# A two-layer hybrid trunk in fp32: step sizes from x itself, head products interleaved in pairs, rotary partner rows copied by DMA

## The reference

```python
h = rmsnorm(x, ln1_g[l]);  proj = h @ w_in[l]
# A: differential attention, 4 heads x 2 components x 64; q and k of each:
q = partial_rope(rmsnorm(q, qk_norm_g[l, 0]), cos, sin)      # k likewise with [l, 1]
def partial_rope(x, cos, sin):                               # first 16 of the 64 dims turn
    x1, x2 = xr[..., :half], xr[..., half:]                  # half = 8
    rot = concat([x1 * c - x2 * s, x1 * s + x2 * c])
    return concat([rot, x[..., ROPE_DIM:]])
# C: S5, a complex diagonal state scan (8 blocks j of 128 states here)
# D: Mamba-2 with 4 heads x 64 and 4 chunks of 128 tokens:
dt = softplus(proj[..., OFF_M2DT:] + dt_bias)                # 4 step sizes per token
y = scores_with_decay @ x_dt + decayed_C @ entering_state    # per head and chunk
y = rmsnorm((y + d_skip * xs) * silu(z), norm_g)
```

## Time and profile before

| | |
|---|---|
| median of 3 runs | 1403.04 us (1402.85 to 1403.28) |
| profiled execution, its own time | 1402.84 us |
| its span | 1401.1 us |
| busy: PE, DVE, POOL, ACT | 1354.3, 924.5, 686.2, 503.7 us |
| granted TensorE clock, mean | 0.99 |
| granted clock from 157.5 to 170 us, mean | 0.73 |
| first qk mean product of layer 0 | at 149.46 us |

### The profile page before, as it was taken

One profiled execution on the slowest core, in us unless ns is written; L12 is line 12 of the kernel. 1 busy time (PEld: TensorE's weight loads), 2 busy tenths in 40 slices (PEclk: granted clock), 3 DMA queues, 4 the chain that ended last, 5 costly groups with the idle time before them and its releaser, 6 DMA issues.

```text
span 1401.1 us, 15858 instructions
## 1 busy us (share of the span) xinstructions
PE 1354.3 (97%) x6130; PEld 1058.0 (76%) x6130; DVE 924.5 (66%) x1239; ACT 503.7 (36%) x754; POOL 686.2 (49%) x370
## 2 busy tenths in 40 slices
PE   7999998899999999999999999989999999999999
PEld 4877566677788888888878765657778888888887
DVE  8879987666788506776237798966577772177730
ACT  5432334655332212323334324445562322123221
POOL 2836897114444444444456378941244444444442
PEclk9999999999999999999999999999999999999999
DMA  6321111113333322323233211111132333233332
GB/s 218 96 61 61 60 48 51 34 42 84 104 93 104 119 78 91 104 91 114 81 108 95 69 46 60 60 46 30 40 113 91 103 104 103 81 95 102 96 111 94
DMA packets 34091, 118.43 MB, mean 85 GB/s; under 512 B 3936, under 2 KB 4064, under 8 KB 34016
## 3 DMA queue, kind: packets, MB, share of 16 engines
q1 hardware_dynamic: 34016, 117.42, 26.6%
HBM read 114.26 MB, written 2.10 MB: 83 GB/s over the span
## 4 chain that ended last, share of the span: by engine, by line
PE 88%; DVE 9%; ACT 1%; issue 1%; POOL 1%; DMA 0%; SPq 0%; DVEq 0%; POOLq 0%
PE bank L423 26%; PE bank L436 25%; PE bank L428 24%; PE bank L490 1%; PE bank L425 1%; PE bank L636 1%; PE bank L499 1%; PE bank L465 1%; PE bank L595 1%; PE bank L597 1%; PE bank L617 1%; PE bank L627 1%; PE bank L449 1%; DVE bank L1055 1%; DVE ml L1061 1%
## 5 line engine op out<-in xcount | busy, mean ns | idle before, releaser
L318 POOL TENSOR_TENSOR wl<-raw,wh 128x1024 fp32r<-128x1024 f32 (+3 forms) x208 | 501.2, 2410 | 633.1 <-ACT wh L771 390.7
L423 PE MATMUL bank<-xl,wh 128*128 128x512 f32 x1152 | 303.3, 402 | 1.7 <-DVE xl L1022 1.1
L771 ACT ACTIVATE wh<-raw 128x1024 fp32r<-128x1024 f32 (+3 forms) x208 | 218.5, 1051 | 236.3 <-PE bank L428 204.1
L436 PE MATMUL bank<-xh,wl 128*128 128x512 f32 x1152 | 285.9, 390 | 0.0
L428 PE MATMUL bank<-xh,wh 128*128 128x512 f32 x1120 | 277.7, 390 | 0.0
L423 PEld LDWEIGHTS bank<-xl,wh 128*128 128x128 f32 x1152 | 215.7, 190 | 72.7 <-issue 25.3
L436 PEld LDWEIGHTS bank<-xh,wl 128*128 128x128 f32 x1152 | 216.0, 188 | 45.1 <-issue 0.3
L428 PEld LDWEIGHTS bank<-xh,wh 128*128 128x128 f32 x1120 | 211.2, 189 | 44.3
L1065 DVE TENSOR_TENSOR x<-x,bank 128x512 f32<-128x512 f32 x64 | 44.0, 688 | 225.1 <-PE bank L436 225.1
L423 PE MATMUL bank<-ml,wh 128*128 128x512 f32 x512 | 139.9, 401 | 0.0
L436 PE MATMUL bank<-mh,wl 128*128 128x512 f32 x512 | 127.5, 389 | 0.0
(11 more groups left out here) (275 smaller groups left out, 1497.2 us busy)
## 6 DMA issues: line engine op xcount, KB each, us to landing
raw<-in_w_gu SPq DMA_DIRECT2D x88, 512.0 KB, 3.5
raw<-in_w_in SPq DMA_DIRECT2D x52, 512.0 KB, 3.5
raw<-in_w_dn SPq DMA_DIRECT2D x32, 704.0 KB, 4.1
raw<-in_w_oe SPq DMA_DIRECT2D x16, 384.0 KB, 3.0
raw<-in_w_ol SPq DMA_DIRECT2D x16, 256.0 KB, 2.6
x<-in_x SPq DMA_DIRECT2D x8, 256.0 KB, 6.8
raw<-in_w_first SPq DMA_DIRECT2D x4, 512.0 KB, 4.8
out_x<-x SPq DMA_DIRECT2D x8, 256.0 KB, 5.1
```

The costliest lines, as they stand in the source:

```text
L318: tt(wl[:, p, 0:cols], raw[:, p, 0:cols], wh[:, p, 0:cols].bitcast(F32), ALU.subtract).then_inc(wl_full, 1)
L423: mm(bank[b][:, :], wh[:, p, k * P:(k + 1) * P], lo[:, k, :], start=(k == 0), stop=False)
L436: w = mm(bank[b][:, :], wl[:, p, k * P:(k + 1) * P], hi[:, k, :], start=False, stop=(k == K - 1))
L771: fn(wh[:, p, 0:cols], raw[:, p, 0:cols], ACT.Copy).then_inc(wh_full, 1)
```

## The change

dt now comes from unsplit fp32 x: `wdt` holds g1 times the weight, padded with zeros to 32 columns, and the eight products go to four column groups of bank 5; a 0/1 matrix `pick` adds the groups in the turn. `m2_apply` works on a pair of heads, one in each half of the columns, products of the two in turn: heads 0 and 1 after unit 12, heads 2 and 3 in the middle of unit 15 (`beside`). `m2_pair(l, 1)` and ACT's square for it move from s = 14 to s = 15. The q and k weights are reordered on the host so that the rotary rows of both components lie on partitions 48 to 79 with partners next to each other. SP copies them swapped from G into `partner[t % 2]`, two DMAs of 16 rows for each t, queued ahead of a weight load. DVE clears the two buffers and copies the sine table to bank 5 once in a layer; the rotary sum is then made in bank 4, where the mean stood, so it waits for ACT's Ln.

```diff
 SP, in weights(g):
+                s = g % (len(UNITS) // L) - 4
+                if 16 <= s < 24:
+                    sp.wait_ge(unit_out, unit_out_of(g // (len(UNITS) // L), s))
+                    for to, of in ((0, 1), (1, 0)):
+                        sp.dma_start(partner[s % 2][ROT0 + to:ROT1:2, :],
+                                     G[ROT0 + of:ROT1:2, s % 2, :]).then_inc(partner_in[s % 2], 16)
                 sp.dma_start(raw[:, g % 2, 0:cols], src[l, i]).then_inc(raw_full[g % 2], 16)
 PE:
-                for n, (a, b) in enumerate(((wdth, xl), (wdth, xh), (wdtl, xh))):
-                    for k in range(KD):
-                        w = mm(bank[5][0:M2H, :], a[:, k, :], b[:, k, :], start=(n == k == 0),
+                for k in range(KD):
+                    r = SH * (k % 4)
+                    w = mm(bank[5][r:r + SH, :], wdt[:, k, :], x[:, k, :], start=(k < 4), stop=(k >= 4))
...
-                    w = nc.tensor.transpose(bank[5][:, t * M2H:(t + 1) * M2H], G[0:M2H, 5, t * P:(t + 1) * P],
+                    w = mm(bank[5][:, t * M2H:(t + 1) * M2H], G[:, 5, t * P:(t + 1) * P], pick, start=True, stop=True)
...
+            def m2_apply(i):
+                pe.wait_ge(mix_ready, nth(mix_ready, 2))
...
+                heads = [(2 * i + e, slice(M2P * e, M2P * e + M2P), *m2buf[e]) for e in range(2)]
+                    for h, r, decayed, _ in heads:
+                        w = mm(bank[5][r, c], xbt[:, t, i, r], decayed[:, c], start=True, stop=(t == 0))
...
 PE, qk_mean(t):
-                claim(4, act_free[4])
+                claim(4, qk_done)
                 mm(bank[4][:, :], block1, G[:, 2, :], start=True, stop=True).then_inc(act_bank[4], 1)
-                claim(5, qk_done)
-                mm(bank[5][:, :], permg[:, t % 2, :], G[:, t % 2, :], start=True, stop=True).then_inc(dve_bank[5], 1)
 PE, beside(s):
-                    if s == 11:
-                        m2_apply(0)
+                    if s == 14:
+                        m2_apply(1)
 DVE, qk_finish(l, t):
                 own(stt(q, G[:, p, :], par_of(l, "qkg", p), cosT, MUL, MUL))
-                dve.wait_ge(dve_bank[5], nth(dve_bank[5]))
-                after(tt(bank[5][:, :], bank[5][:, :], sinT, MUL))
-                after(tt(bank[5][:, :], q, bank[5][:, :], ADD))
+                dve.wait_ge(partner_in[p], 32 * (4 * l + t // 2 + 1))
+                dve.wait_ge(act_free[4], nth(act_free[4]))
+                after(stt(bank[4][:, :], partner[p], par_of(l, "partg", p), bank[5][:, :], MUL, MUL))
+                after(tt(bank[4][:, :], q, bank[4][:, :], ADD))
                 dve.wait_ge(qk_rms, nth(qk_rms))
-                tt(q, bank[5][:, :], G[:, 3 + p, :], MUL).then_inc(qk_done, 1)
+                tt(q, bank[4][:, :], G[:, 3 + p, :], MUL).then_inc(qk_done, 1)
 DVE, s == 15:
+                        nc.vector.memset(partner[0], 0.0)
+                        nc.vector.memset(partner[1], 0.0)
+                        dve.wait_ge(yz_ready, 2 * (l + 1))
+                        own(copy(bank[5][:, :], sinT))
```

More of the change, by code:

```diff
@@ L20 @@
 ROPE = 16
+ROT0, ROT1 = QK - ROPE, QK + ROPE
 THETA = 500000.0
@@ L45 @@
 CONSTS, _o = {}, 0
-for _name, _n in [("ident", P), ("ones", P), ("tri", P), ("perm", P), ("block", P), ("cap", P)]:
+for _name, _n in [("ident", P), ("ones", P), ("tri", P), ("block", P), ("cap", P), ("pick", 4)]:
     CONSTS[_name] = slice(_o, _o + _n)
@@ L148, in build @@
         hst = sb("hst", [P, NQ - 1, M2H, M2P])
+        wdt = sb("wdt", [P, KD, SH], at=offsets["hst"])
         rot = sb("rot", [P, L, 2, SJ, NT])
         rho_all = sb("rho_all", [P, L, SJ])
-        permg = sb("permg", [P, 2, P])
+        partner1 = sb("partner", [P, T], at=offsets["hst"])
+        partner = (G[:, 5, :], partner1[:, :])
         par_all = sb("par_all", [P, L, NPAR])
@@ L207, in build @@
         em_full, em_high, mixed_ready = sem("em_full"), sem("em_high"), sem("mixed_ready")
+        partner_in = [sem(f"partner_in{p}") for p in range(2)]
         sqk_ready, qk_rms, qk_done, v_ready = [sem(n) for n in ("sqk_ready", "qk_rms", "qk_done", "v_ready")]
@@ L1076, in parameters @@
             def parameters(l):
-                w = par_of(l, "wdt", 0, KD * M2H)
-                copy(flat(wdth[:]), w)
+                w = par_of(l, "wdt", 0, KD * M2H).rearrange("p (k h) -> p k h", k=KD)
+                after(nc.vector.memset(wdt[:, :, :], 0.0))
+                gain = par_of(l, "g1", 0, KD).unsqueeze(2).broadcast_to([P, KD, M2H])
                 ts(par_of(l, "subg"), par_of(l, "subg"), par_of(l, "oneml"), None, MUL)
+                ts(par_of(l, "partg"), par_of(l, "partg"), QK ** -0.5, None, MUL)
                 after(ts(par_of(l, "qkg"), par_of(l, "qkg"), QK ** -0.5, None, MUL))
[L1081 to L1085, removed]
+                tt(wdt[:, :, 0:M2H], w, gain, MUL).then_inc(wdt_ready, 1)
             def dt_scaled():
                 dve.wait_ge(dve_bank[5], nth(dve_bank[5]))
-                tt(G[0:M2H, 5, :], bank[5][0:M2H, :], rbc[0:M2H, :], MUL).then_inc(dve_free[5], 1)
+                tt(G[:, 5, :], bank[5][:, :], rbc[:, :], MUL).then_inc(dve_free[5], 1)
                 freed(dve_free[5])
@@ L1567, in _ @@
                         residual(o, o % 2)
+PAIRS = [d for i in range(ROPE // 2) for d in (i, i + ROPE // 2)]
+PLAIN = list(range(ROPE, QK))
+QK_ROWS = [(0, d) for d in PLAIN + PAIRS] + [(1, d) for d in PAIRS + PLAIN]
 def constants():
@@ L1580, in constants @@
     half = ROPE // 2
-    for b in range(2):
-        for i in range(half):
-            lo, hi = b * QK + i, b * QK + half + i
-            perm[hi, lo], perm[lo, hi] = -1, 1
-            cos[lo], cos[hi] = np.cos(ang[:, i]), np.cos(ang[:, i])
-            sin[lo], sin[hi] = np.sin(ang[:, i]), np.sin(ang[:, i])
-    c[:, CONSTS["perm"]] = perm
+    for row, (_, dim) in enumerate(QK_ROWS):
+        if dim < ROPE:
+            cos[row] = np.cos(ang[:, dim % half])
+            sin[row] = np.sin(ang[:, dim % half]) * (-1 if dim < half else 1)
     c[:, CONSTS["block"]] = r[:, None] // QK == r[None, :] // QK
+    c[:, CONSTS["pick"]] = r[:, None] % SH == np.arange(M2H)[None, :]
     c[:, CONSTS["cap"]] = np.where(r[None, :] >= r[:, None], 0.0, NEG)
@@ L1606, in layout @@
     for h in range(HEADS):
-        order += [w[:, :, h * P:(h + 1) * P], w[:, :, a + h * P:a + (h + 1) * P]]
+        rows = np.array([h * P + c * QK + d for c, d in QK_ROWS])
+        order += [w[:, :, rows], w[:, :, a + rows]]
     w_in = units(np.concatenate(order + [w[:, :, b:c]], axis=2))
@@ L1626, in layout @@
     put("g2", tiled(inp["ln2_g"]))
-    put("qkg", np.tile(inp["qk_norm_g"], (1, 1, 2)).transpose(0, 2, 1))
+    dims = np.array([d for _, d in QK_ROWS])
+    put("qkg", inp["qk_norm_g"][:, :, dims].transpose(0, 2, 1))
+    partner = np.where(dims < ROPE, (dims + ROPE // 2) % ROPE, dims)
+    put("partg", inp["qk_norm_g"][:, :, partner].transpose(0, 2, 1))
     put("subg", tiled(inp["subln_g"]))
```

48 lines of the change are left out of this document (19 added, 29 removed).

## The result

The changed kernel takes 1407.13 us (1406.01 to 1409.33), the kernel before 1403.05 in the same comparison: the ratio, estimated from all runs of both, is 1.0032, 95% interval 1.002 to 1.0044. It is 4 us slower, where I had forecast 11 us faster.

A forecast was written before the change was run, and what follows sets the result against it. PE bounds the kernel (97% busy), but DVE nearly fills the rotary stretch. Step sizes 3.1 plus 2.6 us from there on make 5.7 a layer, 11.4 in both: 1391.6 us forecast, own range 1388 to 1396, wider range 1383.5 to 1400.

The forecast's parts named there:

- dt: Input projection: eight plain fp32 products in four column groups take two rounds, 2.0 us, replacing 24 products of 5.56 us.
- the pair of heads: After unit 12: two heads' products, partly side by side in two column halves, take 1.9 us; bounds 1.67 and 3.34.
- the wait before `s5_in(2)`: Scan's second projection: PE arrives about 2 us before DVE's `s5_back(1)` has ended and waits.
- the second mean product's wait: Second rotary step: PE waits about 5 us for the last operation of DVE's `qk_finish(0)`; before, it waited 2.37 us.
- The permutation product: Rotary stretch: sixteen products removed, 6.9 us of PE time a layer, given no gain because DVE becomes the bound.
- DVE's convolutions start with the end of unit 3 and move along: Layer 0, behind the step sizes: DVE's convolutions follow PE's earlier finish, so the 3.1 us gain is kept.
- The price of a late copy: Rotary stretch, odd t: DVE ready at 200.0, copy landed at 200.9; two units take 17.4 us, 0.5 slower than before.
- partners in time: Rival, rotary stretch: copies never hold DVE, a pair takes 16.5 us, gain there 4.4 instead of 2.6, 1388.0 us; chance 0.19.
- First `qk_done`: Start of the rotary stretch: DVE's first `qk_done` comes 2.2 us earlier than the 161.2 before.
- the step sizes: Input projection of each layer: shorter products less a longer `dt_turn`, 5.56 - 2.0 - 0.5, net 3.1 us earlier.
- The clock: Rival: one more clock fall a layer behind PE's waits costs, say, 2.2 us, giving 1396; chance 0.13.
- The pairs: Heads in pairs, units 12 to 17: unit 17 starts about 2.5 us earlier; 1.1 if pairs do not overlap.

## Why the prediction was wrong

- **Prices of the PE work: right.** dt 1.9 us (2.0 forecast; four column groups do run side by side, and the estimate of 2.4 us for them was too high), the turn 0.8 (+0.5 net), the pair of heads 1.9 (1.9), the wait before `s5_in(2)` 1.78 (2), the second mean product's wait 5.0 (5). The permutation product was given nothing, and that holds: with the copies early, the kernel without it takes 1386.6 us and the one with it 1386.1. Those two differ in more than this product (the second also has the held-up pair for `permg`), so a small price could hide there.
- **"DVE's convolutions start with the end of unit 3 and move along": this step failed, and cost some 7 us.** They did start earlier (unit 3 is scaled at 43.02 us instead of 46.07), but small operations then fell beside POOL's `wl`, and unit 4 is scaled at 54.13 instead of 54.40. I had looked at POOL for what it delivers, never for what DVE does at the same time; the trace of before held one such case on DVE, the product that took 2.21 us at 51.95 where its twin took 0.28. The Trainium skill states this case ("SBUF — State Buffer", section "SBUF: two separate sides"): a VectorE operation with two SBUF inputs, or in its two-port mode, and a GpSimd operation take turns at a shared pair of ports, the first has it for its whole length, and the other is blocked. The starts and ends of the rows above agree with it, and I had not weighed it. In layer 1, which has no setup operations there, unit 11 came 3.2 us earlier, as forecast (3.1).
- **The price of a late copy: the size was wrong, by some 9.5 us.** The chain over a pair was nearly right (17.76 us measured between two odd partner products, 17.4 forecast; landing 1.8 us from each issue), and SP was late for the reason given. But I counted the wait as 0.9 us a pair, because I took DVE's work from the earlier trace rows with a cosine product of 1.55 us at odd t, itself slowed beside POOL; it takes 0.94 us at its new time. The pair without the wait is then 15.87 us and not 16.5, the wait 1.9 us (2.5 in layer 0 at t = 7), and behind it the clock falls at unit 25 (9.4 us instead of 7.1). The rival "partners in time" gave 1388.0 us, 3.6 less than the forecast; measured, timely copies are worth 13 us. Adding: 1391.6 + 7 + (13 - 3.6) = 1408, and 1407.1 was measured. That it comes out so near is partly luck, since the errors of the next points are not in this sum. With both causes out, 1386.6 us stands against the rival's 1388.0.
- **First `qk_done` 2.2 us earlier: failed**, in part for the first reason again. In layer 0 the setup operations had taken the 3.1 us of the step sizes, and DVE scaled unit 17 at 151.80 us, only 1.0 earlier than before. Then two low halves and a cosine product took 6.2 us instead of 4.2 beside POOL. Counted from the dt products, it came 1.0 us later than before. In layer 1 it came 3.0 us earlier, where this term and the 3.1 us of the step sizes made 5.3.
- **The clock** had a chance of 0.13 at 2.2 us a layer. Such falls came, in more places than one, behind PE's waits; filling those waits took 8.7 us off the change. With both causes out, the two fills that were tried gained nothing. The fall behind the second mean product stayed in the kernel with early copies, and its price is not known.
- **The pairs** were worth 9 us alone and not 5, since I stopped at unit 17 and did not carry the 2.2 us to the wait of the earlier trace rows, which they remove with the slow clock behind it.

What stays open. How much of the late copies' 13 us is the waits themselves (12.4 us) and how much the clock behind them was not parted; filling the waits overlaps with both. The 7 us of the setup operations are not all delay beside POOL either: at their old place they also took some 1.6 us of DVE's time by their undisturbed lengths, and the hold-up of 2.21 us stood there before the change. That DVE is held by POOL only when its own operands lie in SBUF fits the rows shown here, but it was not tried by itself.

## What to carry to other kernels

- When work moves in time, look at what the *other* engines do beside its new place. Here a gain of 3 us on PE was lost to three DVE operations of 0.2 to 0.6 us that landed beside POOL's. One-time setup belongs where the engine idles.
- A copy on a queue shared with loads is as late as the waits ahead of it. Put it ahead of any wait that it does not need.
- If the engine with the most work waits for another, price a delay by the pair of engines over a whole period, and try each part of a change alone: here one part was worth 9 us and another ate it.

## What the hardware showed unexpectedly

A DVE operation of 0.2 us took 2.44 us beside a POOL subtraction, and ended with it: how much this costs a small operation, I had not expected. Eight fp32 products of 512 tokens in four column groups took 1.85 us (29.00 to the next unit at 30.85), against 0.96 us for one on the full width. And work that nobody reads made a kernel 8.7 us faster, where it filled PE's waits; with both causes out, such fills gained nothing.
